# Six projection units whose first half is also computed in three rounded passes, with its low part written back into the ring

## The reference, cut to what matters

```python
mod = jax.nn.silu(c) @ mod_w + mod_b                 # 1024 x 6144
h = rms_norm(x, g_pre_mix) * (1 + scale1) + shift1
(sc_b, sc_c, sc_x, q, k, v, z, xbc, dt_raw, gl_a, gl_b, gl_c) = split_columns(h @ w_in)
y_a = short_conv_mixer(sc_b, sc_c, sc_x, sc_conv_w) @ w_sc_out
y_b = stick_breaking_attention(q, k, v) @ w_sb_out
y_c = mamba2_mixer(z, xbc, dt_raw, ...) @ w_ssm_out
merged = sigmoid(gl_a) * y_a + sigmoid(gl_b) * y_b + sigmoid(gl_c) * y_c
```

## Time and profile before

| | |
|---|---|
| median of 3 runs | 1266.0 us (1263.57 to 1266.04) |
| the profiled execution | 1261.2 us, its span 1259.5 us |
| granted TensorE clock, mean of the span | 0.962 |
| PE busy | 1115.5 us, 89% |
| DVE busy | 858.5 us, 68% |
| ACT and POOL busy | 478.9 and 479.3 us, 38% each |
| chain that ended last | PE 58%, DMA 27%, DVE 8%, ACT 4% |
| POOL front_lo, L1424 | 19 operations, 62.8 us, mean 3309 ns |
| DVE sums at L1603 | 294 operations, 123.4 us, mean 495 ns |

### The profile page before, as it was taken

How to read it: one execution, slowest core, us unless ns; L and a number is a source line. 1 busy time by engine, 2 the same in 40 slices (tenths; PEclk the granted TensorE clock), 3 DMA queues, 4 the chain that set the end, 5 groups by cost and what they waited for, 6 DMA issues and landing times.

```text
span 1259.5 us, 14756 instructions
## 1 busy us (share of the span) xinstructions
PE 1115.5 (89%) x4718; PEld 730.6 (58%) x4718; DVE 858.5 (68%) x1927; ACT 478.9 (38%) x1110; POOL 479.3 (38%) x355
## 2 busy tenths in 40 slices
PE   3999999989999997999899999887876878788776
PEld 3999899749999996864565555333322323233222
DVE  6675566555888888554986866858668577585454
ACT  2235341053333335532544444433433434334344
POOL 0253432032554461401354465454543535444410
PEclk8999999989999998999899999898999988989999
DMA  9756666553776772571999999999999999999994
GB/s 379 279 217 272 249 245 239 188 229 135 310 279 276 302 322 112 173 296 73 392 405 404 422 421 421 421 421 420 422 421 421 422 421 422 421 420 422 422 421 188
DMA packets 57230, 413.08 MB, mean 328 GB/s; under 512 B 6480, under 2 KB 6480, under 8 KB 7120
## 3 DMA queue, kind: packets, MB, share of 16 engines
q0 software_dynamic: 40608, 295.19, 57.0%
q1 hardware_dynamic: 16416, 116.88, 23.8%
q10 hardware_dynamic: 144, 0.26, 0.1%
HBM read 411.26 MB, written 1.05 MB: 327 GB/s over the span
## 4 chain that ended last, share of the span: by engine, by line
PE 58%; DMA 27%; DVE 8%; ACT 4%; issue 2%; POOL 0%; SPq 0%; DVEq 0%; ACTq 0%; POOLq 0%
PE ps L1036 15%; DMA areaB<-in_experts,idx 11%; PE ps L493 7%; PE ps L495 7%; PE ps L494 7%; DMA ring<-in_experts,idx 6%; DMA gate_area<-in_experts,idx 6%; PE ps L534 4%; PE ps L480 4%; DMA small<-in_experts,idx 3%; PE ps L752 2%; PE ps L598 2%; PE ps L947 2%; DMA areaB<-in_mod_w 2%; PE ps L460 1%
## 5 line engine op out<-in xcount | busy, mean ns | idle before, releaser
L1356 ACT ACTIVATE act<-now 128x1 f32<-128x1 f32 x256 | 50.9, 199 | 260.2 <-DVE now L2111 258.0
L1036 PE MATMUL ps<-areaB,mod_sum 128*128 128x512 f32 x248 | 123.1, 627 | 23.6 <-ACT mod_sum L1363 23.6
L1444 POOL TENSOR_TENSOR w_lo<-ring,w_hi 128x512 fp32r<-128x512 f32 x41 | 101.0, 2477 | 63.6 <-ACT w_hi L1131 63.4
L1603 DVE SCALAR_TENSOR_TENSOR mod_sum<-mod_ring,cols,mod_sum 128x256 f32<-128x256 f32 x294 | 123.4, 495 | 0.0
L493 PE MATMUL ps<-hT_h,w_lo 128*128 128x256 f32 x416 | 118.5, 285 | 5.0 <-POOL hT_l L1451 4.0
L495 PE MATMUL ps<-hT_h,w_hi 128*128 128x256 f32 x416 | 118.6, 285 | 0.0
L1493 POOL DMA_INDIRECT areaB<-in_experts,idx x62 | 69.4, 1119 | 128.5 <-DVE idx L2048 61.5
L494 PE MATMUL ps<-hT_l,w_hi 128*128 128x256 f32 x416 | 117.4, 282 | 0.0
L1036 PE MATMUL ps<-ring,mod_sum 128*128 128x512 f32 x204 | 99.8, 623 | 14.7 <-ACT mod_sum L1363 14.7
L1363 ACT ACTIVATE mod_sum<-small,act 128x128 f32<-128x128 f32 x256 | 102.8, 401 | 24.3 <-PE ps L1036 0.7
L1614 DVE TENSOR_TENSOR w_lo<-ring,w_hi 128x1536 fp32r<-128x1536 f32 x41 | 85.5, 2107 | 31.9 <-ACT w_hi L1131 31.9
(11 more groups left out here) (384 smaller groups left out, 2390.6 us busy)
## 6 DMA issues: line engine op xcount, KB each, us to landing
ring<-in_stream SPq DMA_DIRECT2D x75, 1024.0 KB, 6.1
mod_ring<-in_mod_w POOLq DMA_DIRECT2D x24, 1024.0 KB, 6.4
mod_ring<-in_mod_w SPq DMA_DIRECT2D x18, 1024.0 KB, 6.0
gate_area<-in_mod_w SPq DMA_DIRECT2D x3, 1024.0 KB, 13.5
areaB<-in_mod_w SPq DMA_DIRECT2D x3, 1024.0 KB, 23.4
gate_area<-in_stream SPq DMA_DIRECT2D x3, 1024.0 KB, 13.1
mod_ring<-in_stream SPq DMA_DIRECT2D x2, 1024.0 KB, 11.3
small<-in_small SPq DMA_DIRECT2D x1, 1352.0 KB, 28.4
```

What stands on the lines that cost most here:

```text
L1036: last = mm(ps[:, B3 + 2 * t + b, :], spread_w[n // FEW % 2][:, n % FEW, :], row[ROW_OF[n]][:, D + 512 * b:D + 512 * b + 512], start=first ...
L1444: nc.gpsimd.tensor_tensor(w_lo[s][:, HALF:], slot[s][:, HALF:], w_hi[s][:, HALF:].bitcast(F32), ALU.subtract).then_inc(lo_pool, 1)
L1603: ins = V.scalar_tensor_tensor(out=o[n], in0=w, scalar=vec[:, k:k + 1], in1=o[n], op0=ALU.mult, op1=ALU.add)
```

## The change

Six units, `WHOLE`: qk1 (7), v0 (8), z1 (10), gl2 (13), gl5 (16) and gl7 (18), do their first half in three rounded passes too, 48 passes and no plain product. For this

- hT's first half is split as well: `hq_first[0]` by ACT behind `split_front(FRONT0)`, `hq_first[1]` by POOL ahead of its work for unit 6; both lie in the last third of `gate_area`;
- ACT rounds the first half of such a unit into `whole_hi` (in `diag` and `gate_row`, alternating) right ahead of the second half's rounding; for the third and later ones it also waits until the one that had the same place has been used;
- POOL writes the low part of the first half back into the ring's slot, over the weights themselves, ahead of the second half's;
- TensorE waits for the low part at the start of such a unit (`whole_parts`);
- `sb` rounds the start that it notes for a buffer up to 32 bytes.

```diff
+WHOLE = [AT["qk", 1], AT["v", 0], AT["z", 1], AT["gl", 2], AT["gl", 5], AT["gl", 7]]
...
-            start[name] = nc.sbuf_base
+            start[name] = (nc.sbuf_base + 31) // 32 * 32
...
+        whole_hi = [rounded("whole_hi0", "diag", 0, 2, UNIT // 4), rounded("whole_hi1", "gate_row", 0, 2, UNIT // 4)]
+        hq_first = [rounded(f"hq_first{n}", "gate_area", 2 * UNIT + n * 4 * T, 4, T) for n in range(2)]
...
             def front_parts(u):
 
-                if u == FRONT0:
-                    pe.wait_ge(hq_lo_ready, 1)
+                pe.wait_ge(hq_lo_ready, 1)
                 pe.wait_ge(front_lo_ready, u - FRONT0 + 1)
                 return front_hi[u % 2], front_lo[u % 2]
+
+            def whole_parts(u):
+
+                pe.wait_ge(hq_lo_ready, 2)
+                pe.wait_ge(whole_lo_ready, WHOLE.index(u) + 1)
+                return whole_hi[WHOLE.index(u) % 2], lo_whole[u]
...
+                if u in WHOLE:
+                    whole = whole_parts(u)
                 for b in range(2):
                     for k in range(4):
...
+                        if u in WHOLE:
+                            mm3(o, [v[:, b, k * P:(k + 1) * P] for v in whole], [v[:, k, :] for v in hq_first], start, False,
+                                skip_group_check=True)
+                        else:
+                            mm(o, w[:, at:at + P], hT[:, k, :], start=start, stop=False, skip_group_check=True)
...
                 act.wait_ge(unit_done, u - 1)
+                if u in WHOLE:
+                    n = WHOLE.index(u)
+                    if n >= 2:
+                        act.wait_ge(unit_done, WHOLE[n - 2] + 1)
+                    A(whole_hi[n % 2], half_unit(u, 0), ACT.Identity).then_inc(whole_hi_ready, 1)
                 A(front_hi[u % 2], second_half(u), ACT.Identity).then_inc(front_hi_ready, 1)
...
             split_front(FRONT0)
+            A(hq_first[0], hT[:, 0:4, :], ACT.Identity).then_inc(hq_hi_ready, 1)
...
             for u in range(FRONT0, FRONT1):
+                if u == FRONT0 + 2:
+                    pool.wait_ge(hq_hi_ready, 2)
+                    nc.gpsimd.tensor_tensor(hq_first[1], hT[:, 0:4, :], hq_first[0].bitcast(F32), ALU.subtract)\
+                        .then_inc(hq_lo_ready, 1)
+                if u in WHOLE:
+                    n = WHOLE.index(u)
+                    pool.wait_ge(whole_hi_ready, n + 1)
+                    nc.gpsimd.tensor_tensor(lo_whole[u], half_unit(u, 0), whole_hi[n % 2].bitcast(F32),
+                                            ALU.subtract).then_inc(whole_lo_ready, 1)
                 split_front(u)
```

More of the change, by code:

```diff
@@ L184, in build, with half_unit @@
                + [query_w[0], mT_flat[:, :]] + query_w[1:] + [hT_flat[:, :]])
+        def half_unit(u, half):
+            if u == AT["v", 0]:
+                return cut(slot[u % RING], half * UNIT // 2, 2, UNIT // 4)
+            return slot[u % RING].rearrange("p (b h n) -> p b h n", b=2, h=2)[:, :, half, :]
         def second_half(u):
-            if u == AT["v", 0]:
-                return cut(slot[u % RING], UNIT // 2, 2, UNIT // 4)
-            return slot[u % RING].rearrange("p (b h n) -> p b h n", b=2, h=2)[:, :, 1, :]
+            return half_unit(u, 1)
         def mod_place(m):
@@ L249, in build, with whole_lo @@
         hq_h, hq_l = rounded("hq_h", "mT", 0, 4, T), rounded("hq_l", "mT", 4 * T, 4, T)
+        whole_hi = [rounded("whole_hi0", "diag", 0, 2, UNIT // 4), rounded("whole_hi1", "gate_row", 0, 2, UNIT // 4)]
+        hq_first = [rounded(f"hq_first{n}", "gate_area", 2 * UNIT + n * 4 * T, 4, T) for n in range(2)]
+        def whole_lo(u):
+            name, at = f"whole_lo{u}", u % RING * UNIT
+            if u == AT["v", 0]:
+                return rounded(name, "ring", at, 2, UNIT // 4)
+            v = nc.alloc_sbuf_tensor_at(name, [P, UNIT], F32R, offset=start["ring"] + 4 * at)
+            return v[:, :].rearrange("p (b h n) -> p b h n", b=2, h=2)[:, :, 0, :]
+        lo_whole = {u: whole_lo(u) for u in WHOLE}
         hT_h, hT_l = rounded("hT_h", "mT", 0, KC, T), rounded("hT_l", "hT", 0, KC, T)
@@ L319, in build @@
         front_hi_ready, front_lo_ready = sem("front_hi_ready"), sem("front_lo_ready")
+        whole_hi_ready, whole_lo_ready = sem("whole_hi_ready"), sem("whole_lo_ready")
         at_s, at_max, at_exp, at_p, at_T, at_pT, at_pv, at_o = (
@@ L530, in proj_T @@
                     return
+                if u in WHOLE:
+                    whole = whole_parts(u)
                 for b in range(2):
                     for k in range(4):
-                        at = (b * KC + k) * P
-                        mm(ps[:, bank, b * T:(b + 1) * T], w[:, at:at + P], hT[:, k, :], start=(b == 0 and k == 0),
-                           stop=False, skip_group_check=True)
+                        at, o, start = (b * KC + k) * P, ps[:, bank, b * T:(b + 1) * T], b == 0 and k == 0
+                        if u in WHOLE:
[3 more added lines that the diff above has]
+                            mm(o, w[:, at:at + P], hT[:, k, :], start=start, stop=False, skip_group_check=True)
                 both = front_parts(u)
@@ L627, in _ @@
                 proj_T("qk", j)
-            w = arrived("v", 0)
+            arrived("v", 0)
             bank = bank_free()
+            whole = whole_parts(AT["v", 0])
             for t in range(NT):
                 for k in range(4):
-                    mm(ps[:, bank, t * T:(t + 1) * T], hT[:, k, t * P:(t + 1) * P], w[:, k * T:(k + 1) * T],
-                       start=(t == 0 and k == 0), stop=False, skip_group_check=True)
+                    mm3(ps[:, bank, t * T:(t + 1) * T], [v[:, k, t * P:(t + 1) * P] for v in hq_first],
+                        [v[:, k // 2, (k % 2) * T:(k % 2 + 1) * T] for v in whole], t == 0 and k == 0, False,
+                        skip_group_check=True)
             both = front_parts(AT["v", 0])
```

## The result

The changed kernel took 1272.4 us (median of 5, 1270.26 to 1274.31) against 1264.8 (5 runs beside it): ratio 1.0068, interval 1.0053 to 1.0083. The ratio is estimated from all executions; the quotient of the two medians is 1.0060. The forecast was 1266.6 and no measurable change; it is slower by 7.6 us, which is near the 6.8 of rival A.

What follows compares the result with a forecast made beforehand. TensorE, busy 151.24 of 151.46 us, bounds the front part. 3.5 saved against waits of 3.3, 0.3 and 0.4 gave +0.5, rounded to +0.6: 1266.6 us; own range 1264.4 to 1268.5, 8 in 10 1262.6 to 1273.4.

Steps and rivals of the forecast that it cites:

- rival A: At v0: POOL shut out by VectorE's batch of blocks 10 and 11, TensorE waits 9.5; +6.8, 1272.8 us; chance 0.35 with its like.
- TensorE's gain: In the six changed units: 24 rounded passes replace the plain first half, saving 0.58 us each, 3.5 in all.
- C: Passes don't run at 0.12 us with the low part from the ring: +1 to +4; no chance of its own.
- What the added work costs: On ACT and POOL: seven roundings of 1.07 us, seven subtractions from 2.4; each subtraction let in costs VectorE 2.1 us.
- Step 1: hT's low part starts at 61.96 in the conv batch; VectorE slips 2.1, then another 2.1 with POOL let in.
- Step 2: SP's queue: pair 10 and 11 goes out at 73.7 or 75.8, so unit 8 lands at 83.4 or 85.5.
- Step 3: At v0: TensorE waits 1.2 or 3.3 us, and v0 ends 0 or 2.1 later; taken as +2.1.
- Step 4: ACT before the stick-breaking chain: z0's copy-out slips 2.1 + 1.05; 0.3 of z1's saving left; +0.7 at gl7's start.
- Step 5: VectorE before decay: its batch ends at 174.3, gl7 waits 0.4 us; from there to L735 VectorE ties with TensorE.
- The sum: Over the kernel: 3.5 saved against waits of 3.3 at v0, 0.3 at gl0, 0.4 at gl7: +0.5, rounded +0.6.
- the same at gl0: At gl0, where POOL got in at 106.81: POOL shut out instead would cost 3.3 us.
- B: Nobody late at v0, only VectorE's batch before decay holds: about -3.0, 1263.0 us; chance 0.22.

Runs made afterwards that it cites:

- e6_order: Kernel before with the six units' passes on stand-in operands, no added ACT or POOL work, VectorE's batch of blocks 22 and 23 moved: 1260.67 us, ratio 0.9971.
- e7_base: Kernel before with only VectorE's batch of blocks 22 and 23 moved behind the square at the chain's end: 1264.09 us, ratio 0.9994.
- run 32: Not a run or kernel: the words belong to "it had run 32 products of 128x8", TensorE's work just before; no time belongs to it.
- a3_again: The changed kernel run once more, unaltered, one profiled execution: 1277.87 us, against 1266.16 before.
- e3_queue: Changed kernel with the pair of blocks 12 and 13 behind unit 11's load instead of unit 10's in SP's queue: 1267.63 us, ratio 1.0045.
- e11_order: Changed kernel with only VectorE's batch of blocks 22 and 23 moved: 1272.11 us, ratio 1.0062.
- q1_again: Changed kernel with pair 12 and 13 behind unit 11's load and VectorE's batch moved, run once more, one profiled execution: 1275.46 us.
- e1_passes: Changed kernel's TensorE passes on operands already there, without the added ACT and POOL work, against the kernel before: 1261.97 us, ratio 0.9990.
- e2_work: Kernel before plus the added ACT and POOL work alone, low part written over the high one, TensorE as before: 1270.38 us, ratio 1.0046.
- e8_both: Changed kernel with pairs 12 to 21 each one load later and VectorE's batch of blocks 22 and 23 moved: 1267.64 us, ratio 1.0027.
- e9_five: Changed kernel with five whole units (gl2, gl3, gl4, gl5, gl7), late low part of hT, batch 22 and 23 moved: 1268.55 us, ratio 1.0035.
- e10_three: Changed kernel with three whole units (gl2, gl5, gl7), late low part of hT, batch 22 and 23 moved: 1262.77 us, ratio 0.9986.
- e12_two: Changed kernel with pair 12 and 13 behind unit 11's load and VectorE's batch of blocks 22 and 23 moved: 1262.24 us, ratio 1.0007.

## Why the prediction was wrong, by its own steps

**TensorE's gain** held. The table above has -0.61 for qk1, v0, gl2 and gl5 (0.58 forecast), and `e6_order` shows the sum: 3.8 us saved, 3.5 forecast. C is ruled out by the table, where the low part does come from the ring; the passes of `e6_order` read none from there.

**What the added work costs** held in its rate, about 2.1 us of VectorE for each POOL operation that gets in; what failed is the count of VectorE work that it meets. I followed it through the conv batch and the batch of blocks 8 and 9, and took the dt chain and the short convolution behind it as a few stalls (the batch of blocks 10 and 11 from some 86.7 on). In the profile after these alone fall behind by 6.1 us: the batch of blocks 8 and 9 starts 3.84 later than before (70.18 against 66.34), that of 10 and 11 9.93 later. That I did not go by the lock of the Trainium skill, "SBUF — State Buffer", section "SBUF: two separate sides", as giving a loser its turn after one instruction, was right: at 72.59 POOL was shut out again to the end of the batch, and its subtraction took 5.46 us instead of 2.36, while VectorE's steps take 0.4.

**Step 1** held in both courses as far as the conv: hT's low part starts at 63.66, 61.93 without the late start, and conv ends at 67.6 (forecast 62.0 and 67.6). That POOL then gets in holds in the v0 course, and not in the profile after, where sc1 at 0.79 moves the request. The same fall of the clock is in an execution without the change, `e7_base`, the stretch from 64 to 68 us:

```profile
64.00:68.00 4.00, 4.00 (x13) 3.21 (x12) 3.96 (x10) 0.00 (x0) 0.34 (x1) 0.57 0.07 27
```

So it isn't the change's doing, but with the change it goes with the course. TensorE was busy throughout in both; just before, it had run 32 products of 128x8, and it ran them before too, where the clock stayed at 1.00.

**Step 2** held for what it looked at: the pair at 75.8 or 73.7 (78.97 - 3.15 = 75.8 in `a3_again`, 75.43 - 1.73 = 73.7 after). In the profile after unit 8 landed at 83.6, forecast 83.4 for that case. In `a3_again` it landed at 87.1 instead of 85.5, since the landing took 11.3 us from the pair and not 9.7. The step stopped at this pair. The next one, 12 and 13, has unit 11's load behind it, and waits for a batch that ends 14.2 us later than before: 1.7 of it is the start, 2.1 the conv batch, 6.1 the dt chain and the short convolution, 4.3 the batch itself. This is the step that failed in the profiled course: 6.7 us of waiting and, behind the idle time, 2.7 us of clock in gl0. `e3_queue` shows it: with one entry moved the wait is gone.

**Step 3** is the term that was mis-sized in the other course. It gave v0 3.3 us of waiting and +2.1 at its end; measured 5.1 (4.7 and 4.8 in `e11_order` and `q1_again`) and +6.75. The wait is longer by the 1.6 of the landing and 0.2 more. The rest, 2.8 us, is the clock after the idle, which no term of the sum had. A rule of the Trainium skill, "TensorE: Matmul & The Clock Gate", section "Part 1: The HAM clock gate (the "warmup" mystery)", would have named it: the gate follows how busy TensorE has been lately. The trace agrees, 0.50 behind 5.14 us of idle time.

**Step 4** can be read only in part. After, z0's copy-out is 0.78 later than v0's was (2.98 against 2.20), where I had 1.05 for ACT's rounding ahead of the chain. z1's own saving cannot be seen, since its copy-out waits for ACT, which waits for unit 11's load.

**Step 5** failed at another place than it looked. In the profile after TensorE waits for nobody at the decay (forecast 0.4); in the v0 course it waits 0.2 to 1.9 there, and 2.4 to 4.2 at L715 ahead of it, behind unit 17's late load, which no step had. But at the last norm, which I had as a tie with 0.22, TensorE waits 2.2 in the profile after, because POOL is let into the batch of blocks 22 and 23 (7.72 us instead of 5.62). `e1_passes` has the same without any added work and `e2_work` without any saved pass, so either of the two is enough for it; where the batch is moved, the wait is gone.

**The sum:** on the terms of the profiled pair, from 1261.2 to 1272.4: start 1.7, sc1's clock 1.7, gl0 6.7 + 2.7, last norm 2.0, passes -3.6, which is 11.2. The start and the clock of sc1 are not the change's: `e7_base`, before with one batch moved, has both (sc0 at 60.03, clock 0.57). The medians differ by 7.6. **Rival A** had the size (+6.8, 1272.8) and the place wrong: it saw POOL shut out at v0, and "the same at gl0" at 3.3. The profiled course is the other way round: POOL gets in, VectorE is late, and TensorE waits for a transfer behind another in SP's queue. **B**, nobody late, came about with six units only in `e6_order`, which has none of the added work.

Open: why sc1's clock falls in some executions, why unit 8's landing took 11.1 to 11.3 us in the v0 course, and how the wait at the decay in `e8_both` and `e9_five` divides between late pairs and POOL's share in VectorE's batches; no kernel was run that parts them.

## What to carry to other kernels

Work that is added to an engine with idle time is paid by whoever shares something with it: follow it through the next engine's whole order, and through every queue entry that waits for that engine, to what stands behind this entry. Count an idle time of TensorE with the clock that follows it, here 2.7 us on top of 6.7. Added POOL work cost nothing that could be measured where nobody waited for VectorE (`e10_three`), and where a course depends on who asks first, one profile shows only one of them.

## What the runs showed that I had not expected

- **One program, two courses.** `e12_two` has executions about 1262 and about 1273 us. The fork is where POOL's request falls in a 0.4 us step of VectorE at about 70 us.
- **When POOL is let in.** VectorE's multiply-adds come every 0.395 us. At the fork, the batch of blocks 8 and 9, the requests of the 18 traces go by where they fall in such a step: the four at 0.31 to 0.32 us got in (2.39 us), the 14 at 0.03 to 0.05, 0.14 to 0.16 and 0.38 to 0.39 were shut out to the end of the batch. It is no rule for the other batches. Among the first requests in all batches up to 225 us, 21 of 86 at 0.00 to 0.23 got in, and 20 of 33 at 0.30 to 0.36. So the place in the step alone doesn't decide, and what else does stays open.
- **Clock after idle.** 6.7 us of waiting gave gl0 a clock of 0.71 over 9.06 us, in place of 6.3 us at 1.00; 5.1 us gave v0 0.50 for 6 us.
- **A transfer's landing.** The load of unit 8 stands right behind a pair in SP's queue. It landed 9.7 us after the pair's issue before, 9.7 to 10.0 in the six traces of the other course, and 11.1 to 11.3 in the three traces of the v0 course.
